# Projection chunks in another order, and separate score banks for attention's first unit

## The reference, cut to what matters

```python
h  = modulate(rmsnorm(x, g_pre_mix), sh1, sc1)          # 1024 latent tokens
hc = modulate(rmsnorm(ctx, g_pre_mix), csh1, csc1)      # 256 context tokens
dq, dk, dv, gq, gk, gv = split(h @ w_in)                # 512, 512, 512, 512, 128, 128 columns
gq, gk = rmsnorm(gq, q_norm_g), rmsnorm(gk, k_norm_g)   # per head of 64
dq, dk, gq, gk = (rope_2d(v, ang_row, ang_col) for v in (dq, dk, gq, gk))
# the same for hc, which gives keys and values only
o_diff = rmsnorm(attend(dq1, dk1, dv) - lam * attend(dq2, dk2, dv), subln_g) * (1 - lam_init)
o_gqa  = attend(gq, gk, gv)                             # 8 query heads, 2 key heads
# attend: softmax(q @ k.T / 8) @ v over all 1280 keys
```

## Time and profile before

| | |
|---|---|
| median of 3 runs | 2013.47 us (2008.12 to 2016.77) |
| the profiled execution | 2011.13 us, of which its span is 2009.4 us |
| PE busy | 1846.7 us, 92% of the span |
| DVE, ACT, POOL busy | 64%, 55%, 38% |
| the front | from 0 to some 355 us |
| attention | from 355.5 to some 839 us |
| the tail | from 839 us to the end |

### The profile page before, as it was taken

One profiled execution on the slowest core, in us unless ns is written; L12 is line 12 of the kernel. 1 busy time (PEld: TensorE's weight loads), 2 busy tenths in 40 slices (PEclk: granted clock), 3 DMA queues, 4 the chain that ended last, 5 costly groups with the idle time before them and its releaser, 6 DMA issues.

```text
span 2009.4 us, 42261 instructions
## 1 busy us (share of the span) xinstructions
PE 1846.7 (92%) x12486; PEld 978.7 (49%) x12487; DVE 1279.1 (64%) x2155; ACT 1110.6 (55%) x1520; POOL 765.6 (38%) x1115
## 2 busy tenths in 40 slices
PE   4899989798999999898988999998979999999995
PEld 1687767565666666576643333333323333333332
DVE  2854275455888855565553777775747777777766
ACT  2432121465666656522323777776756777777772
POOL 1101010220111111034453566664655666666652
PEclk8999999799999999999989999999999999999998
DMA  8365345444344232179435889798999889899985
GB/s 288 119 173 190 122 127 145 104 103 119 77 115 105 54 89 40 54 216 152 109 92 195 292 293 342 240 339 295 328 317 359 282 302 351 283 349 357 333 241 207
DMA packets 154071, 416.80 MB, mean 207 GB/s; under 512 B 22177, under 2 KB 77345, under 8 KB 129105
## 3 DMA queue, kind: packets, MB, share of 16 engines
q1 hardware_dynamic: 94466, 302.87, 43.1%
q0 software_dynamic: 49808, 95.89, 20.1%
q10 hardware_dynamic: 9712, 16.99, 2.6%
HBM read 351.50 MB, written 83.67 MB: 217 GB/s over the span
## 4 chain that ended last, share of the span: by engine, by line
PE 42%; DMA 10%; issue 2%; DVE 2%; SPq 1%; ACT 1%; POOL 1%; POOLq 0%; DVEq 0%; ACTq 0%
PE ps_rg L2193 20%; PE ps_d L2209 10%; DMA w_experts_down<-in_w_exp_down 5%; PE ps_y L2177 3%; PE ps_rg L2121 2%; PE ps_y L2102 2%; DMA w_experts_gate_up<-in_w_exp_up 2%; PE ps_d L2140 1%; DMA x_in<-in_tokens 1%; PE ps_rg L2219 1%; DMA y_scratch<-e_y,e_target_index 1%; PE ps_d L2102 1%; SPq L1357 1%; DMA gathered<-h_scratch,e_gather_index 1%; PE ps_rg L2196 0%
## 5 line engine op out<-in xcount | busy, mean ns | idle before, releaser
L2193 PE MATMUL ps_rg<-weight_slabs,gatheredT 128*32 128x512 f32 x3456 | 511.6, 596 | 0.1
L2196 PE MATMUL ps_rg<-w_experts_gate_up,gatheredT 128*32 (+1 forms) x1152 | 510.6, 596 | 0.0
L1963 DVE COPY weight_slabs<-w_experts_gate_up 128x1024 f32 x576 | 384.1, 727 | 53.6 <-PE ps_rg L2193 42.1
L1703 ACT ACTIVATE weight_slabs<-w_experts_gate_up 128x1024 f32 x288 | 304.5, 1058 | 91.5 <-PE ps_rg L2193 50.2
L2193 PEld LDWEIGHTS ps_rg<-weight_slabs,gatheredT 128*32 128x32 f32 x3456 | 135.8, 110 | 314.8 <-issue 304.2
L1971 DVE COPY weight_slabs<-w_experts_down 128x1024 f32 x288 | 188.4, 698 | 154.1 <-PE ps_rg L2193 120.7
L2209 PE MATMUL ps_d<-weight_slabs,e_actT 128*32 128x512 f32 x1728 | 263.3, 599 | 19.2 <-DVE weight_slabs L1971 17.0
L990 DVE TENSOR_REDUCE neg_max<-ps_scores 128x1 f32<-128x1280 f32 x128 | 190.1, 1489 | 133.0 <-PE ps_scores L1091 132.7
L2213 PE MATMUL ps_d<-w_experts_down,e_actT 128*32 x576 | 262.1, 598 | 0.0
L1709 ACT ACTIVATE weight_slabs<-w_experts_down 128x1024 f32 x144 | 152.1, 1058 | 50.4 <-PE ps_rg L2193 46.7
L948 ACT ACTIVATE probs<-ps_scores,neg_max 128x1280 f32<-128x1280 f32 x96 | 127.6, 1330 | 94.2 <-DVE neg_max L990 94.1
(11 more groups left out here) (327 smaller groups left out, 3119.4 us busy)
## 6 DMA issues: line engine op xcount, KB each, us to landing
w_experts_gate_up<-in_w_exp_gate SPq DMA_DIRECT2D x64, 1024.0 KB
w_experts_gate_up<-in_w_exp_up SPq DMA_DIRECT2D x64, 1024.0 KB
w_experts_down<-in_w_exp_down SPq DMA_DIRECT2D x64, 1024.0 KB
w_mod_later<-in_w_mod ACTq DMA_DIRECT2D x32, 512.0 KB, 4.7
w_mod_first<-in_w_mod SPq DMA_DIRECT2D x4, 2048.0 KB, 16.1
w_in_raw<-in_w_in SPq DMA_DIRECT2D x32, 256.0 KB, 4.3
y_scratch<-in_k_zeros SPq DMA_DIRECT2D x16, 512.0 KB
values<-in_tokens SPq DMA_DIRECT2D x10, 512.0 KB, 11.9
```

Of the source, the lines that this page charges most:

```text
L1703: act.activation(slab[:, (v + j) % SLABS, 0].rearrange("p (a m) -> p a m", a=2), gate_up_part(ring_gu, gate_up_slot(w), j), ACT.Copy).then ...
L1963: last = nc.vector.tensor_copy(slab[:, (v + j) % SLABS, q - 1].rearrange("p (a m) -> p a m", a=2), gate_up_part(ring_gu, gate_up_slot(w), j))
L2193: last = nc.tensor.matmul(psR[tile(q)], xT[m][:, k, tile(q)], W, start=(k == 0), stop=(k == KD - 1))
L2196: last = nc.tensor.matmul(psR[tile(0)], xT[m][:, k, tile(0)], gate_up_chunk(ring_gu, slot, k), start=(k == 0), stop=(k == KD - 1))
```

## The change

The chunk of differential values moves from the third place to the last. The order becomes k (n = 0 to 9), kv (10 to 19), normed queries (20 to 27), plain queries (28 to 35), values (36 to 45). The unit that POOL waits for is now `first_of[2]`, again the first of the normed queries. Work that hangs on n stays at its n.

In attention, unit 0 puts its odd rows at column 1536, as the "d" units do, so that its even rows have banks 0 to 2 and its odd rows banks 3 to 5. As bank 5 is also where `tr(0, 0)` writes, the first transposes into banks 5 and 6 now wait for all four exponentials of unit 0.

```diff
-    CH = [(512, 512, "k", 0), (2048, 256, "kv", 8), (1024, 512, "v", 0), (1536, 512, "q", 8), (0, 512, "q", 0)]
+    CH = [(512, 512, "k", 0), (2048, 256, "kv", 8), (1536, 512, "q", 8), (0, 512, "q", 0), (1024, 512, "v", 0)]
...
-            ready = turned.index(first_of[3]) + 1
+            ready = turned.index(first_of[2]) + 1
...
+    def own_banks(u):
+        return u == 0 or units[u][0] == "d"
+
     def span(u, r):
-        base = 0 if r % 2 == 0 else 3 * 512 if units[u][0] == "d" else KEYS
+        base = 0 if r % 2 == 0 else 3 * 512 if own_banks(u) else KEYS
         return slice(base, base + KEYS)

     def third_bank(u, r):
-        return 5 if units[u][0] == "d" and r % 2 else 2
+        return 5 if own_banks(u) and r % 2 else 2
...
                 g = last_in_bank(u, kt)
                 if g is not None:
                     wait_out(pe, g)
+                else:
+                    pe.wait_ge(s_e, n_rows(0))
```

## The result

| | median | runs |
|---|---|---|
| before | 2012.41 us (2004.92 to 2016.77) | 8 |
| changed | 1999.81 us (1995.74 to 2002.58) | 8 |

The ratio is 0.9938, with a 95% interval from 0.9917 to 0.9959: 12.6 us by the medians. The profiled execution of the changed kernel has a span of 1994.9 us (before 2009.4).

The account below looks back on a forecast made before the run. Two chains of single steps bound the seam and attention's first score rows; elsewhere in the front mostly PE. The terms -9.2 + 1.1 + 0.5 - 5.4 = -13.0 us gave 2000.5 us, with 1995.5 to 2008.0 for 8 in 10.

Parts of the forecast that it names:

- The seam: From the last projection to attention's first score: 1.3 us in place of 10.5, so 9.2 us saved (8.5 to 9.3).
- Three turns: Three PE turns from the old gap now stand ahead of the last projection, 0.36 us each: 1.1 us lost.
- DVE's lag: DVE starts the normed queries later but has fewer operations before slice 2: 0.5 us lost (-0.2 to 1.4).
- The new hand-over, plain queries to values: Where values follow plain queries, PE finds weight slices 2 and 6 ready, 3.0 and 1.0 us to spare: no cost.
- The banks: Attention's first score rows: two rounds in place of four up to the fifth maximum, 5.4 us saved (4.2 to 6.5).
- The added wait: Attention's first transposes wait for all four exponentials of unit 0: costs nothing, 0.3 us at most.
- The rule on the clock: In the first score rows the lower clock holds, as PE is mostly idle: total gain 1.2 us smaller.
- only the seam counts: In attention, unit 1 waits for queries that POOL loads: only -7.6 us, 2005.9 us; chance 0.10.
- The seam's gap isn't the store's: PE's idle time before the first score may hide something else; up to 4 us come back: 2004.5 us; chance 0.07.
- DVE's lag is carried on: Stalls of 8.2 us at kv-to-normed and plain-to-values hand-overs: both 2016.9 us, chance 0.03; one 2008.7 us, chance 0.09.

## Why the prediction was right, point by point

The forecast was 2000.5 us, 13.0 less; measured are 1999.81, 12.6 less by the medians, and 13.9 at the point from which both traces run alike. The nearness of 12.6 to 13.0 says little by itself, as the interval of the ratio, put in time, goes from 8.3 to 16.7 us; the terms say more.

- *The seam*, forecast -9.2: 10.49 to 1.09 us, **-9.4**. The steps are those that were named. The hand-over from the last engine's end to the first score took 0.45 us (347.74 to 348.19), less than the 0.65 and the 0.55 of the rows it was taken from. The kernel with the values fourth shows the same term from the other side.
- *Three turns*, forecast +1.1, and *DVE's lag*, +0.5: together **+1.0**, by the stretch (171.04 against 170.04; 170.86 and 170.91 in the two other kernels with this order). The prediction had PE pay for the lag once, with the wait at slice 2; the trace has two waits for turns beside it in both kernels, and the three together grew by 0.5 (5.63 to 6.10), the forecast's number. That leaves another 0.5 for the turns and all else, where 1.1 was forecast. The higher clock behind the long wait (0.50 before, 0.66 changed, 0.58 in the second profile of the changed kernel) works in that direction; how much of it that is, no run separates. From DVE's start on the normed queries (179.38) to slice 2 (232.79) it was 53.4 us; 52.9 was forecast, and 54.2 was before.
- *The new hand-over, plain queries to values*, forecast at nothing with 1.0 us to spare at slice 6. No wait of PE is there. DVE's subtraction of slices 6 and 7 starts at 287.87, and PE's unit ends at 293.04, with the first matmul of slice 6 at 291.52: 3 us to spare, as one subtraction takes 0.69. Of the 2 us more than worked out, 1 is the product after n = 35, which the prediction names but doesn't count; the rest wasn't followed. (The terms that it adds up to 9.6 make 9.5.)
- *The banks*, forecast -5.4 as the middle between -4.2 and -6.5: **-6.4** in the first profile, **-5.3** in the second one of the same kernel. (The -6.5 is -6.4 by its own terms, 17.5 less 11.1.) The two rounds in place of four were right, the price of the clock was right by luck: the working put the lower clock on both rounds or on none and took the middle, while the runs show two levels. With the values last and these banks the fifth maximum came 11.18 and 11.21 us after the first score in two executions, 12.25, 12.26 and 12.26 in three others, in which the first round alone was slow. Behind a pair of rows at the lower clock the next rows were at full clock each time.
- *The added wait*, forecast at 0.3 at most: the fourth exponential is out at 359.19 and the transposes start at 359.25, while PE ends unit 1's first row at 359.34 by the modelled end of its matmuls. No wait is to be seen there. With the banks alone it was 0.66 us and with the values fourth 0.44, more than the 0.3, but off the path to unit 1's first exponential.
- *The rule on the clock*, weighed as a loss of 1.2 us. The Trainium skill ("TensorE: Matmul & The Clock Gate", section "What's actually happening") has the throttled clock as the default and activity as what lifts it. The trace agrees where rows come one at a time (0.53 with the order alone) and where the first round was slow (0.66 in the second profile); in the first profile the loss didn't come (1.00).

Of the rivals, *only the seam counts* falls: unit 1's first row started at 357.94 behind an exponential, and POOL had begun with its loads at 348.42. *The seam's gap isn't the store's* falls: of the 1.09 us 0.60 are the copy. *DVE's lag is carried on* falls at both hand-overs, where it has PE wait for 4.0 us each: there is no wait at the values, and at kv's one of 1.57 us (0.57 in the second profile). In the run with the query chunks exchanged the wait followed the normed queries.

What was over the trace's 13.9 in the terms (-9.4 + 1.0 - 6.4 = -14.8) is upstream of the change: unit 20's wait ended at 175.67 in place of 174.81. Of these 0.86 us 0.69 are a longer wait there (1.57 against 0.88). It isn't the new order: the second profile of the same kernel has 174.88, and the other kernels whose PE waits there 174.9 to 176.3. What makes it vary was not followed.

## What to carry to other kernels

Put last in a stage the work whose result is used where it lies; what still has to be turned, stored and waited for belongs ahead of something long. Of a chain that hands one buffer around, count the rounds: two private buffers took four rounds of 3.8 us down to two of 4.5, or to one of 5.6 and one of 4.5, with the steps of DVE and ACT as long as before. A part of that is PE's clock, which was 0.59 before and reached 1.00 with two rows in a row. And when a chunk falls behind on one engine, look at what stands behind its slow work in that engine's list. Here moving four short operations ahead of it was worth 2.5 us more.

## What the runs showed that was not expected

- The clock of the first score rows isn't fixed by the program. The same kernel had its second pair of rows at 1.00 in one execution and at 0.66 in another, after the same 2.55 us of work and a wait of 2.67 or 2.68 us, which makes 1.1 us. What decides between the two is not shown.
- An idle time of 5.68 us before the first score cost less than thought: two rows in a row, 4.6 us of PE's work, ran at 0.50, and after that the clock was full, while rows taken one at a time stayed at 0.53 for 16 us.
- The part of the program that no edit touched, from unit 1's first exponential to the end, took 1634.6 us before, 1634.0 changed, 1629.3 with the order alone and 1641.8 with the query chunks exchanged. The changed kernel's second execution took 1637.3 there, 3.3 more than its first. Its spread, over 12 us, is as large as the change's whole effect. What makes it was not tried; single times of this kernel can't carry a difference of half a per cent.
